# Split weights interleaved in pairs, and 512-column products run from last column to first

## The reference, cut to what matters

```python
def first_block(x, c, ctx, c_ctx, w_ada, b_ada, ...):
    mod_l = (silu(c) @ w_ada + b_ada)              # 2048 x 12288, for c and c_ctx
    h_l = modulate(rms_norm(x, g), sh_a, sc_a)     # 256 x 2048; h_c the same from ctx
    qa, kva, kr, cb, cc, ch = split(h @ w_in)      # 2048 x 3904
    att = block_attention(q, k, v)                 # 8 heads, 512 keys
    conv = cb * dwconv3(cc * ch, conv_w, conv_b)
    x = x + gt_a * (rms_norm(concat(att, conv)) @ w_out)      # 2048 x 2048
    u = dwconv3(modulate(rms_norm(x, g2)) @ w_up)             # 2048 x 11008
    a, g = split(u)
    return rms_norm(x + gt_f * ((a * silu(g)) @ w_down))      # 5504 x 2048

def second_block(x, ...):
    z = rms_norm(x) @ w_in_2                       # 2048 x 10248
    a = moba_attention(...) @ w_proj_a             # 1024 x 2048
    b = forgetting_attention(...) @ w_proj_b       # 1024 x 2048
    x = x + (sigmoid(g_a) * a + sigmoid(g_b) * b) @ w_out_2   # 2048 x 2048
    h = square(relu(rms_norm(x) @ w_up_2))         # 2048 x 8192
    return rms_norm(x + h @ w_down_2)              # 8192 x 2048
```

## Time and profile before

| | |
|---|---|
| median of 3 runs | 2709.5 us (2705.6 to 2710.15) |
| span of the profiled execution | 2701.8 us |
| TensorE matmuls (PE) | busy 2606.8 us, 21322 records |
| weight loads (PEld) | busy 2522.5 us, 21322 records |
| VectorE (DVE) | busy 1758.9 us, 2033 instructions |
| ScalarE (ACT) | busy 1222.5 us, 1487 instructions |
| mean granted TensorE clock | 0.984 of full speed |
| HBM read | 548.53 MB, 204 GB/s over the span |

### The profile page before, as it was taken

How to read it: one execution, slowest core, us unless ns; L and a number is a source line. 1 busy time by engine, 2 the same in 40 slices (tenths; PEclk the granted TensorE clock), 3 DMA queues, 4 the chain that set the end, 5 groups by cost and what they waited for, 6 DMA issues and landing times.

```text
span 2701.8 us, 51009 instructions
## 1 busy us (share of the span) xinstructions
PE 2606.8 (96%) x21322; PEld 2522.5 (93%) x21322; DVE 1758.9 (65%) x2033; ACT 1222.5 (45%) x1487; POOL 112.5 (4%) x196
## 2 busy tenths in 40 slices
PE   6899988989999999999999999999999999999998
PEld 4699877889999999999999999999999999999997
DVE  5989776778888755665865655555665555555554
ACT  6753333345454544444544445444444444434433
POOL 0000323300000000000000110000000000000000
PEclk9899999989999999999999999999999999999999
DMA  9878766757777665565665555666566666666662
GB/s 353 283 227 271 254 210 206 240 174 242 250 242 250 208 198 173 168 220 175 197 189 155 180 159 160 194 194 193 192 183 195 193 195 194 189 194 195 194 210 95
DMA packets 289063, 553.55 MB, mean 205 GB/s; under 512 B 19386, under 2 KB 28712, under 8 KB 288232
## 3 DMA queue, kind: packets, MB, share of 16 engines
q1 hardware_dynamic: 288328, 548.53, 63.8%
q10 hardware_dynamic: 544, 2.29, 0.2%
HBM read 548.53 MB, written 2.10 MB: 204 GB/s over the span
## 4 chain that ended last, share of the span: by engine, by line
PE 84%; DVE 9%; ACT 3%; issue 2%; DMA 1%; POOL 1%; SPq 0%; ACTq 0%; DVEq 0%; POOLq 0%
PE half L1887 25%; PE half L1889 25%; PE half L1888 25%; DVE wlo L1100 4%; DMA raw<-in_w_ada 1%; ACT whi L618 1%; DVE acc L1129 1%; PE half L1921 1%; PE half L1923 1%; PE half L1922 1%; DVE acc L1132 1%; DVE tmp L1213 0%; PE half L2168 0%; PE half L2141 0%; PE half L2140 0%
## 5 line engine op out<-in xcount | busy, mean ns | idle before, releaser
L1100 DVE TENSOR_TENSOR wlo<-raw,whi 128x1024 fp32r<-128x1024 f32 (+1 forms) x909 | 1089.3, 1211 | 777.5 <-ACT whi L618 775.7
L618 ACT ACTIVATE whi<-raw 128x1024 fp32r<-128x1024 f32 (+1 forms) x909 | 940.5, 1048 | 1038.6 <-PE half L1889 922.6
L1887 PE MATMUL half<-hf,whi 128*128 128x256 f32 x2400 | 668.2, 278 | 6.4 <-DVE hf L1192 5.2
L1888 PE MATMUL half<-hf,whi 128*128 128x256 f32 x2400 | 666.2, 278 | 0.0
L1889 PE MATMUL half<-hf,wlo 128*128 128x256 f32 x2400 | 666.2, 278 | 0.0
L1887 PE MATMUL half<-hid,whi 128*128 128x256 f32 x1712 | 475.0, 277 | 1.2 <-DVE wlo L1100 1.2
L1888 PE MATMUL half<-hid,whi 128*128 128x256 f32 x1712 | 474.4, 277 | 0.0
L1889 PE MATMUL half<-hid,wlo 128*128 128x256 f32 x1712 | 474.4, 277 | 0.0
L1887 PEld LDWEIGHTS half<-hf,whi 128*128 128x128 f32 x2400 | 451.3, 188 | 8.5 <-issue 5.8
L1889 PEld LDWEIGHTS half<-hf,wlo 128*128 128x128 f32 x2400 | 453.0, 189 | 0.0
L1888 PEld LDWEIGHTS half<-hf,whi 128*128 128x128 f32 x2400 | 452.1, 188 | 0.0
(11 more groups left out here) (290 smaller groups left out, 3020.4 us busy)
## 6 DMA issues: line engine op xcount, KB each, us to landing
raw<-in_w_up SPq DMA_DIRECT2D x288, 512.0 KB, 4.3
raw<-in_w_in SPq DMA_DIRECT2D x216, 512.0 KB, 4.0
raw<-in_w_down SPq DMA_DIRECT2D x212, 512.0 KB, 4.5
raw<-in_w_ada SPq DMA_DIRECT2D x192, 512.0 KB, 5.2
raw<-in_w_out SPq DMA_DIRECT2D x64, 512.0 KB, 4.8
raw<-in_w_proj_a SPq DMA_DIRECT2D x16, 512.0 KB, 4.5
raw<-in_w_proj_b SPq DMA_DIRECT2D x16, 512.0 KB, 4.2
raw<-in_w_up SPq DMA_DIRECT2D x16, 384.0 KB, 3.4
```

What stands on the lines that cost most here:

```text
L618: A(whi[:, s, 0:elems], raw[:, c, 0:elems], ACT.Copy).then_inc(s_hi_ready, 1)
L1100: V.tensor_tensor(wlo[:, s, 0:elems], raw[:, c, 0:elems], whi[:, s, 0:elems].bitcast(F32), ALU.subtract).then_inc(s_drained, 1)
L1887: mm(o, hi, x[:, 0:T], start=(k == 0 and b % 2 == 0), stop=False, skip_group_check=True)
L1888: mm(o, hi, x[:, T:2 * T], start=False, stop=False, skip_group_check=True)
```

## The change

It touches where elements lie and in which order they are read; the computation and the instructions are the same ones. In the issue order of all five engines nothing changes place and nothing is added or taken out: beside line numbers, only the shapes of the splits differ (128x1024 becomes 128x4x2x128).

First, `woven` lays a chunk out in `whi` and `wlo` so that two neighbouring blocks of 128 columns are interleaved: column n of the even block at element 2n, column n of the odd block at 2n + 1, within 256 elements. ScalarE and VectorE read `raw` in straight runs of 128 and write every second element; VectorE also reads `whi` with that step. `woven_block` picks one block out of the pair, so the weight load steps by two elements. Chunks whose size isn't a multiple of 512 elements (the narrow products) and those passed `split_straight` (for `rows`, `token_product`, `key_values`) keep the old layout. Second, in products of width 512, `block` turns the moving tile and the accumulator around (`[:, ::-1]`): both are walked from column 255 down to 0, so that each output lands where it did.

```diff
@@ helpers
+        def woven(t, s, elems):
+            return t[:, s, 0:elems].rearrange("p (a n q) -> p a q n", n=P, q=2)
+
+        def straight(t, c, elems):
+            return t[:, c, 0:elems].rearrange("p (a q n) -> p a q n", n=P, q=2)
+
+        def woven_block(w, at):
+            pair = w[:, at - at % (2 * P):at - at % (2 * P) + 2 * P].rearrange("p (n q) -> p q n", q=2)
+            return pair[:, at // P % 2, :]
@@ ScalarE
-            def split(elems):
+            def split(elems, weave=True):
...
-                A(whi[:, s, 0:elems], raw[:, c, 0:elems], ACT.Copy).then_inc(s_hi_ready, 1)
+                if weave and elems % GW == 0:
+                    A(woven(whi, s, elems), straight(raw, c, elems), ACT.Copy).then_inc(s_hi_ready, 1)
+                else:
+                    A(whi[:, s, 0:elems], raw[:, c, 0:elems], ACT.Copy).then_inc(s_hi_ready, 1)
...
+            def split_straight(elems):
+                split(elems, False)
...
-                ahead(STD, turn if g > 0 else None, side={...})
+                ahead(STD, turn if g > 0 else None, split=split_straight, side={...})
...
-            ahead(KVB, turn)
+            ahead(KVB, turn, split=split_straight)
@@ VectorE
-                V.tensor_tensor(wlo[:, s, 0:elems], raw[:, c, 0:elems], whi[:, s, 0:elems].bitcast(F32),
-                                ALU.subtract).then_inc(s_drained, 1)
+                if weave and elems % GW == 0:
+                    V.tensor_tensor(woven(wlo, s, elems), straight(raw, c, elems), woven(whi, s, elems).bitcast(F32),
+                                    ALU.subtract).then_inc(s_drained, 1)
+                else:
+                    V.tensor_tensor(wlo[:, s, 0:elems], raw[:, c, 0:elems], whi[:, s, 0:elems].bitcast(F32),
+                                    ALU.subtract).then_inc(s_drained, 1)
@@ TensorE
-            def block(o, b, hi, lo, x, k, nk):
-
-                mm(o, hi, x[:, 0:T], start=(k == 0 and b % 2 == 0), stop=False, skip_group_check=True)
-                mm(o, hi, x[:, T:2 * T], start=False, stop=False, skip_group_check=True)
-                return mm(o, lo, x[:, 0:T], start=False, stop=(k == nk - 1), skip_group_check=True)
+            def block(o, b, hi, lo, x, k, nk, back=False):
+
+                xh, xl = x[:, 0:T], x[:, T:2 * T]
+                if back:
+                    o, xh, xl = o[:, ::-1], xh[:, ::-1], xl[:, ::-1]
+                mm(o, hi, xh, start=(k == 0 and b % 2 == 0), stop=False, skip_group_check=True)
+                mm(o, hi, xl, start=False, stop=False, skip_group_check=True)
+                return mm(o, lo, xh, start=False, stop=(k == nk - 1), skip_group_check=True)
...
+                part = woven_block if width == GW else (lambda w, at: w[:, at:at + P])
...
-                            ins_ = block(folded(half(nth))[:, b, :], b, hi[:, at:at + P], lo[:, at:at + P], src(k), k, nk)
+                            ins_ = block(folded(half(nth))[:, b, :], b, part(hi, at), part(lo, at), src(k), k, nk, width == GW)
```

More of the change, by code:

```diff
@@ L748, in _ @@
             for g in range(8):
-                ahead(STD, turn if g > 0 else None, side={c: replies[GC * g + c] for c in range(GC) if GC * g + c in replies})
+                ahead(STD, turn if g > 0 else None, split=split_straight, side={c: replies[GC * g + c] for c in range(GC) if GC * g + c in replies})
             def norm_both():
@@ L866, in _ @@
             ahead(QBG, lambda: conv_in(0), split=split_pair)
-            ahead(KVB, turn, side={0: q_root()})
+            ahead(KVB, turn, side={0: q_root()}, split=split_straight)
             ahead(STD, lambda: turn(2), None, CONV_SUMS[1])
             ahead(QBG, lambda: conv_in(1), split=split_pair)
-            ahead(KVB, turn)
+            ahead(KVB, turn, split=split_straight)
             ahead(STD, lambda: turn(2), None, CONV_SUMS[2], side={6: att1})
@@ L1013, in _ @@
                 ahead(STD, turn, side={2: roots()} if s == 0 else side[1])
-                ahead(STD, turn, side=side[2])
+                ahead(STD, turn, side=side[2], split=split_straight)
                 if s == 1:
@@ L1272, in _ @@
             for g in range(8):
-                ahead(STD, mod_rows if g > 0 else None, (lambda: mod_cols(4 * g - 4)) if g > 0 else None,
+                ahead(STD, mod_rows if g > 0 else None, (lambda: mod_cols(4 * g - 4)) if g > 0 else None, split=split_straight,
                       side={c: replies[GC * g + c] for c in range(GC) if GC * g + c in replies})
@@ L1520, in _ @@
             ahead(QBG, lambda: conv_in(0), split=split_pair)
-            ahead(KVB, lambda: queries(0), side={0: q_root()})
+            ahead(KVB, lambda: queries(0), side={0: q_root()}, split=split_straight)
             ahead(STD, lambda: first_values(0), mod, CONV_SUMS[1], side={5: rotate(0)}, third=(1, lambda: keys(0)))
             ahead(QBG, lambda: conv_in(1), split=split_pair)
-            ahead(KVB, lambda: queries(1))
+            ahead(KVB, lambda: queries(1), split=split_straight)
             ahead(STD, lambda: first_values(1), mod, CONV_SUMS[2], side={5: rotate(1), 6: att1}, third=(1, lambda: keys(1)))
@@ L1527, in _ @@
             ahead(QBG, lambda: conv_in(3), split=split_pair, side={1: att1})
-            ahead(KVB, lambda: queries(2))
+            ahead(KVB, lambda: queries(2), split=split_straight)
             def both(*parts):
@@ L1536, in _ @@
             ahead(QBG, lambda: conv_in(5), split=split_pair, side={1: att1})
-            ahead(KVB, lambda: queries(3))
+            ahead(KVB, lambda: queries(3), split=split_straight)
             ahead(WIDE, lambda: first_values(3), None, WIDE_SUMS,
@@ L1730, in _ @@
                       (lambda: norm_x(0 if s == 0 else 3)) if s < 2 else None,
-                      side={} if s == 0 else {1: before, 4: before})
+                      side={} if s == 0 else {1: before, 4: before}, split=split_straight)
                 if s == 1:
```

## The result

The changed kernel takes 2757.49 us (median of 4 runs, 2754.97 to 2758.64) against 2707.55 us for the kernel before on the same chip (2701.8 to 2710.15): a ratio of 1.0183, 95% interval 1.0168 to 1.0197. The forecast was 2687 us, faster. The time lies in the range; the sign is wrong, and the rival "the other way, slower" (2765 us) came nearest.

The account below looks back on a forecast made before the run. PE's matmuls were taken to bound the kernel, so their pitch counts. Losing the long pitch gave -22 us, weight load, walk direction and splits 0: 2709.5 - 22 = 2687 us, range 2600 to 2768 us.

Parts of the forecast that it names:

- the other way, slower: Rival on the matmul pitch in `block`: the long pitch becomes the rule, +56 us, 2765 us; chance 0.17.
- What bounds the kernel: Whole kernel: it lasts as long as its matmuls take; PE is never idle from 600 to 2686 us.
- the long one's price: Matmuls in `block`: the long pitch, 4.3 ns over the short, was taken to cost 24 us now.
- the long pitch goes: Likeliest case, matmuls in `block`: the changed walk and layout remove the long pitch, -22 us, 2687 us; chance 0.32.
- Accumulators downwards, price 0: 512-column products in `block`: writing accumulators last column to first was taken to neither gain nor lose.
- The rival at half pace: Rival: weight load, moving read or accumulator write takes one element instead of two; pitch 215, +1.9 ms; chance 0.07.
- Weight load with a step of two, price 0: Weight loads in `block`: stepped read taken as free, hidden under the matmul before with a cover of 5 ns.
- Splits, price 0: ACT and DVE splits writing with a step of two: 0 to 0.8 us a chunk, 784 woven chunks, taken as 0.
- The long pitch becomes the rule: Same rival as "the other way, slower": 128 stepped weights meet the moving read more often, +56 us, 2765 us; chance 0.17.
- The pitch itself falls: Rival on matmuls in `block`: streams out of each other's way, pitch about 109 ns, 2610 us; chance 0.24.

Follow-up runs that it names:

- e2: Kernel before with only the walk changed: moving tiles and accumulators of 512-column products read last column to first, weights straight; 2754.49 us, ratio 1.0201.
- e4: Kernel before with only the moving tiles of the 512-column products read last column to first, accumulators forwards; 2757.36 us, ratio 1.0201.
- e10: Kernel before with only the walk turned around, and 8 weight columns in each block's second and third matmul; 2758.53 us, one run.
- e5: Kernel before with only the accumulators of the 512-column products written last column to first; 2708.61 us, ratio 1.0005.
- e13: Kernel before with 64 unused bytes behind the split weights, so moving tiles and weights stand alike modulo 128 bytes; 2791.88 us, ratio 1.0330.
- e3: Kernel before with weights of four blocks interleaved, so loads step by four floats, walk forwards; 4912.14 us, ratio 1.8174.
- e7: Kernel before with 64 instead of 128 weight columns in the second and third matmul of each block; 2688.18 us, one run.
- e12: Kernel before with the second and third matmul of each block exchanged; 2706.77 us, ratio 0.9997.
- e11: Kernel before with 32 unused bytes ahead of the split weights and 32 behind, operands 96 bytes apart modulo 128; 2766.89 us, ratio 1.0212.
- e15: Kernel before with the split weights 64 bytes further, so weights and moving tiles stand alike modulo 128 bytes; 2791.85 us, ratio 1.0336.
- e18: Kernel before with the split weights 16 bytes past a multiple of 128, moving tiles unmoved, 48 bytes apart; 2738.78 us, ratio 1.0142.

## Why the prediction was wrong

*What bounds the kernel.* Right, and it carried the comparison: the loss lies behind 600 us, in the pitch, in full. That the kernel has two pitches was right too. The prediction put the long one's price at 24 us; the run with half loads gained some 20.

*"The two streams no longer walk the same way over adjacent words. I forecast that the long pitch goes"*, for -22 us. This is the step that failed. It took a pattern that no row had, a downward moving read, and gave it the better of two pitches because the change alters how the reads meet. The runs show the opposite. The downward moving read brings the long pitch nearly everywhere, 117.5 ns and +50 us (e2, e4), and keeps it with 8 weight columns beside two of three matmuls (e10), so it rests little on the meeting of the reads that the step argued from. The prediction says of the short pitch that "nothing in the rows ties it to a direction". The same held for the long one, and was a reason to keep both ends, +4.3 ns as likely as -4.3; the chance of 0.32 against 0.17 had no row behind it. Priced from the rows at the other end the sum would have been 2765 us, 0.3% from the result.

*Accumulators downwards, price 0.* Right (e5, ratio 1.0005). The rival at half pace came true in neither downward pattern.

*Weight load with a step of two, price 0.* Wrong by itself. The load takes 5 ns longer, about the cover of 5 ns that the prediction worked out from the earlier trace rows, and the layout alone makes the pitch 119.8 ns and costs 88 us. That the pitch is long because the cover is used up doesn't follow: straight weights at the bad placement have the same pitch (e13). In the changed kernel this is hidden behind the price of the walk, so the error in this term doesn't show in the sum. Why the two prices don't add stays open: with the load at 194 ns in both, the pitch is 119.8 ns walked forwards and 117.5 downwards.

*Splits, price 0.* The price on the time is right. ACT takes 129 ns more a woven split, DVE 3; even with both at 2.04 us or more (e3) PE waited 1.1 us for them behind 600 us, though at twice the pitch. The trace has 780 woven splits, where the prediction reckoned 784.

*The rivals.* "The long pitch becomes the rule" was right in its size and in the sign of the pitch (+56 us against +50 measured), and wrong in its reason, the stepped weight read: straight weights and a downward walk suffice. That it came so near is in part luck, since its own cause, the layout alone, measures +88 us. "The pitch itself falls" has nothing for it in any run; no window read here has less than 113 ns.

What stays open: what decides, at the placement of the kernel before, between short and long after a stall. It takes full weight reads beside it (e7, one run), its stretches lie elsewhere in another trace (e12), and the short pitch is gone at every other placement tried (e11, e13 to e15, e18). Open too is why a downward read costs what it does.

## What to carry to other kernels

Where PE never waits, take its pitch from counts over windows in several stretches, and ask of any change of pattern or address what it does to the two reads of TensorE; a pattern that no row shows has no sign until it has been run alone. Before rearranging 4-byte operands, try the cheap things one by one: the place of weights and moving tiles to each other within 128 bytes was worth 3.3% here, and a change to the buffers can shift it unnoticed. A price measured at one placement need not hold at another: the downward walk cost 50 us at one and gained 25 at the other. Two changes that each make the stream slower can hide each other, so a pair is judged only by running its halves.

## What the runs showed of the hardware

- fp32r, 256 moving columns, clock 1.00: pitch 113.0 or 117.6 ns straight with operands 64 bytes apart modulo 128, 119.6 ns when they stand alike, and 116.4 to 118.1 at 32, 48 and 96 bytes apart. All these are by window counts, some 0.3 ns low.
- The moving tile read from last column to first: 117.5 ns, with 128, 64 or 8 weight columns loaded beside two of three matmuls; 13 us slower still where the operands stand alike. Accumulators written so: no change.
- Weights with a step of two floats, moving tile read forwards: load 194 ns instead of 188, pitch 119.8 ns at either of two placements. With a step of four: load 325 ns, pitch 234 ns.
- Splits that write with a step of two floats: ACT 1187 ns instead of 1058 (1160 with the layout alone), DVE 1226 instead of 1223. With a step of four: 2067 and 2040.
